# Order of the work around the sparse attention steps of a streaming encoder: minima, scaling, weight splits and gate tanh

## What is computed

```python
def sparse_attend(q, k, v, idx, valid):
    ...
    s = jnp.einsum('bqkgd,bqskd->bqkgs', qg, kg).astype(jnp.float32) * SCALE
    s = jnp.where(valid[:, :, None, None, :], s, NEG)
    p = jax.nn.softmax(s, axis=-1)
    o = jnp.einsum('bqkgs,bqskd->bqkgd', p.astype(v.dtype), vg)
    ...
merged = jax.nn.sigmoid(g_a) * br_a + jax.nn.sigmoid(g_b) * br_b + jax.nn.sigmoid(g_c) * br_c
```

## Time and profile before

| what | value |
|---|---|
| median of three runs | 1905.6 us |
| the profiled execution, its own time | 1904.03 us |
| its span, first to last instruction | 1902.2 us |
| mean granted clock of TensorE | 0.992 |
| busy: TensorE, VectorE, ScalarE, GpSimd | 96%, 57%, 32%, 21% |
| HBM traffic | 50 GB/s over the span |

### The profile page before, as it was taken

One profiled execution on the slowest core, in us unless ns is written; L12 is line 12 of the kernel. 1 busy time (PEld: TensorE's weight loads), 2 busy tenths in 40 slices (PEclk: granted clock), 3 DMA queues, 4 the chain that ended last, 5 costly groups with the idle time before them and its releaser, 6 DMA issues.

```text
span 1902.2 us, 30436 instructions
## 1 busy us (share of the span) xinstructions
PE 1835.3 (96%) x11609; PEld 1784.5 (94%) x11609; DVE 1081.7 (57%) x1749; ACT 606.2 (32%) x1006; POOL 394.8 (21%) x315
## 2 busy tenths in 40 slices
PE   5999999999999997989999999999999999999997
PEld 4899999989999996778899999999999999999997
DVE  5257878967688684778664445553234442244543
ACT  4232122268511225777723221111011111011132
POOL 2112212256533323234420001110001110011100
PEclk9999999999999998999999999999999999999998
DMA  4111111110111113211213111111111111111112
GB/s 144 34 34 48 37 34 50 49 34 24 35 49 50 37 45 100 52 40 46 56 56 136 45 34 55 44 44 44 47 42 44 44 44 55 44 34 44 43 45 92
DMA packets 167457, 96.72 MB, mean 51 GB/s; under 512 B 7676, under 2 KB 163596, under 8 KB 167372
## 3 DMA queue, kind: packets, MB, share of 16 engines
q1 hardware_dynamic: 166396, 93.57, 17.0%
q0 software_dynamic: 976, 2.00, 0.4%
HBM read 89.55 MB, written 5.99 MB: 50 GB/s over the span
## 4 chain that ended last, share of the span: by engine, by line
PE 90%; DVE 4%; ACT 2%; POOL 2%; issue 1%; DMA 1%; SPq 0%; DVEq 0%; ACTq 0%
PE ps L957 75%; PE ps L969 4%; PE ps L1066 3%; PE ps L1089 3%; PE ps L1164 2%; PE ps L1204 2%; DVE probs L2074 1%; POOL probs L829 0%; ACT w_hi L1337 0%; DVE attn_sum L2124 0%; DMA x_rows<-in_x_prompt 0%; POOL w_lo L778 0%; DMA w_raw_in_lo<-in_w_in 0%; PE ps L1030 0%; DVE h_rows L1817 0%
## 5 line engine op out<-in xcount | busy, mean ns | idle before, releaser
L957 PE MATMUL ps<-h_hi,w_hi 128*128 128x352 f32 (+1 forms) x1944 | 424.5, 327 | 3.9 <-POOL w_lo L769 3.9
L957 PE MATMUL ps<-h_hi,w_lo 128*128 128x352 f32 (+1 forms) x1944 | 419.9, 323 | 0.0
L957 PE MATMUL ps<-h_lo,w_hi 128*128 128x352 f32 (+1 forms) x1944 | 419.6, 324 | 0.0
L957 PEld LDWEIGHTS ps<-h_hi,w_hi 128*128 128x128 f32 (+1 forms) x1944 | 330.5, 189 | 6.8 <-issue 5.1
L957 PEld LDWEIGHTS ps<-h_hi,w_lo 128*128 128x128 f32 (+1 forms) x1944 | 333.6, 188 | 0.5
L957 PEld LDWEIGHTS ps<-h_lo,w_hi 128*128 128x128 f32 (+1 forms) x1944 | 330.7, 188 | 0.5
L1337 ACT ACTIVATE w_hi<-w_raw 128x1024 fp32r<-128x1024 f32 (+1 forms) x128 | 124.2, 971 | 245.6 <-PE ps L957 245.5
L926 POOL TENSOR_TENSOR t<-t,t 128x1056 f32<-128x1056 f32 x22 | 54.4, 2472 | 631.4 <-ACT t L1698 631.4
L1895 DVE MAX8 top<-key_mask 128x8 f32<-128x768 f32 (+5 forms) x192 | 170.5, 890 | 11.8 <-PE ps L957 1.1
L769 POOL TENSOR_TENSOR w_lo<-w_raw,w_hi 128x1024 fp32r<-128x1024 f32 (+1 forms) x53 | 100.5, 1896 | 355.1 <-ACT w_hi L1337 355.1
L1895 DVE MATCH_REPLACE8 key_mask<-top,key_mask 128x768 f32<-128x768 f32 (+5 forms) x192 | 167.7, 876 | 0.0
(11 more groups left out here) (261 smaller groups left out, 2975.3 us busy)
## 6 DMA issues: line engine op xcount, KB each, us to landing
w_raw_in_lo<-in_w_in SPq DMA_DIRECT2D x56, 256.0 KB, 2.8
w_raw<-in_w_in SPq DMA_DIRECT2D x54, 256.0 KB, 3.0
w_raw<-in_w_gate SPq DMA_DIRECT2D x44, 256.0 KB, 2.9
w_raw<-in_w_up SPq DMA_DIRECT2D x44, 256.0 KB, 3.0
w_raw<-in_w_down SPq DMA_DIRECT2D x32, 256.0 KB, 2.9
w_raw_in_lo<-in_w_in SPq DMA_DIRECT2D x44, 128.0 KB, 2.2
x_rows<-in_x_prompt SPq DMA_DIRECT2D x8, 512.0 KB, 8.9
w_raw<-in_w_out SPq DMA_DIRECT2D x16, 256.0 KB, 3.0
```

What stands on the lines that cost most here:

```text
L957: last = nc.tensor.matmul(PS[0:rows, NB * k + b, 0:e - a], w[:, k, t, 0:rows], x[:, t, a:e], start=m == 0 and w is WHI and x is hi, stop=m ...
```

## The change

Three loops are reordered; no instruction is added or removed.

- GpSimd: in slot c = 2, the scaling of the next pair (larger tiles) is issued ahead of the slot's weight half.
- ScalarE: within a slot, the splits and the tanh are issued last, behind `normalise`, `low_share` and `exp`. Where a pair has one chunk, both `exp` are issued in slot 0.
- VectorE: for pairs of the smaller tiles (`ahead` is 2), both `mask_max` are issued before the loop over chunks, ahead of `pt_low` and `output`; before, the second one stood in slot 1.

```diff
--- before.py
+++ after.py
@@ -902,10 +902,10 @@
             for y, pair in enumerate(SPARSE):
                 after = SPARSE[y + 1] if y + 1 < len(SPARSE) else None
                 for c in range(max(len(pair["chunks"]), 3)):
+                    if c == 2 and after and after["ahead"] == 1:
+                        normalise(after)
                     if c < len(pair["chunks"]):
                         sparse_split(y, c)
-                    if c == 2 and after and after["ahead"] == 1:
-                        normalise(after)
                 if y > 1:
                     output(SPARSE[y - 2])
             for pair in SPARSE[-2:]:
@@ -1627,15 +1627,18 @@
                     for c in range(max(count, 4)):
                         if c < count:
                             pt_high(pair, c)
-                            sparse_gates(y, c)
                         if c == 0 and after and after["ahead"] == 2:
                             normalise(after, 1)
                         if c == 0 and y > 0 and ps[y - 1]["last"]:
                             low_share(ps[y - 1])
-                        if c < 2 and ahead:
+                        if c < min(count, 2) and ahead:
                             exp(ahead, c)
+                        if c == 0 and count == 1 and ahead:
+                            exp(ahead, 1)
                         if c == 2 and after and after["ahead"] == 1:
                             normalise(after, 1)
+                        if c < count:
+                            sparse_gates(y, c)
                     if y > 0 and ps[y - 1]["last"]:
                         output(ps[y - 1])
                 low_share(ps[-1])
@@ -2147,8 +2150,11 @@
                         if early:
                             invert(after, 0)
                             invert(after, 1)
+                        if ahead and ahead["ahead"] == 2:
+                            mask_max(ahead, 0)
+                            mask_max(ahead, 1)
                         for c in range(max(count, 4)):
-                            if c < 2 and ahead:
+                            if c < 2 and ahead and ahead["ahead"] == 1:
                                 mask_max(ahead, c)
                             if c == 2 and after and not early:
                                 invert(after, 0)
```

## The result

The changed kernel takes 1921.76 us (median of four runs, 1920.9 to 1922.64) against 1905.9 for the kernel before (four runs, the three above and one of 1909.12); the ratio is 1.008 with a 95% interval of [1.0062, 1.0097]. Both the forecast (1908.6) and its range (1900.5 to 1913.5) were missed, on the slow side.

A forecast was written before the change was run, and what follows sets the result against it. TensorE, busy for 96% of the span, was taken as the bound. Smaller tiles 0.3 us gained, larger tiles 3.4 lost: 3.1 us more, put on the median of 1905.6, forecast 1908.6 us; range for 8 in 10 1900.5 to 1913.5.

The forecast's parts named there:

- the clock term of the sum: Sparse stage: a stretch of TensorE at the lower clock after a wait costs about 1.6 us; none counted in the sum.
- the slow rival: Late tanh waits: give-back fails or two to three further lower-clock stretches at 1.6 us each; about 1912.5 us, chance 0.37.
- Part 1: VectorE, smaller tiles, both minima first: at most 9.9 us of minima waits go, 0.3 us gained in all.
- step 9: Smaller tiles: splits of job 8 come late, chunk 1's fill starts at 773.9 as today; the 2.9 us gain is given back.
- step 4: Smaller tiles, before the fill of job 4: a wait of 2.46 us becomes about 2.8 for weights; gain so far 0.6.
- Step 17: Larger tiles: tanh of job 11 behind low share, exponential and split; 2.1 us lost, after give-backs 0.1 gained.
- Step 22: Larger tiles: tanh of job 14 comes behind the second exponential, after the split had moved behind the first; 1.3 us lost.
- Step 28: Larger tiles: tanh of job 19 comes behind an exponential that waits for a minimum; 1.8 us lost.
- Step 20: Larger tiles: half split moves behind an exponential, GpSimd meets it before the scaling, which ends later; 0.35 us lost.
- Steps 29 to 32: Two-chunk pairs, forecast for 29, 30, 31: tanh behind low share, half just ahead of GpSimd's scaling; together 1.55 us lost.
- The fast one: Sparse stage: minima waits go, only tanh waits replace them; 9.9 and 4.9 gained, 5 lost, about 1896 us, chance 0.19.
- The shared pair: VectorE scaling and GpSimd subtraction block each other: 0.76 us more each time; sum takes none, range one or two.

The follow-up runs named there:

- The filler: The changed kernel plus 46 unused TensorE matmuls ahead of the three waits in step 9, other engines' orders left as they are: 1913.44 us.

## Why the prediction was wrong

**The step that failed is the clock term of the sum.** The prediction said that the waits now put in place of others might "bring on further stretches", at 1.6 us each, and left them out of the sum; only the slow rival had them, two or three. There were 20.5 us more at the lower level, worth up to 10.2 us; in steps 9 and 10 alone two stretches of 6.8 us each, where the row covers 3.2. It also had no part for the stretch of 6.8 us near 722, which would have shown that one can last that long. The filler shows the price directly: 5.2 us for those two steps. Of the stage's 17.7 us the forecast had 3.1 (by its own terms 1908.7 us, written as 1908.6); of the 14.6 it lacked, 10.2 are the clock's and 4.4 are waits that were sized too small.

The sign that the prediction named for the slow rival came: the mean granted clock was 0.982 to 0.985 in the four runs, against 0.986 to 0.992 in the 38 runs of the kernel before that stand beside the experiments.

**Right, by their size and place.** Part 1 up to step 9: 2.9 us gained was forecast, and the scores of step 9 come 3.2 us earlier against the stage's start. The wait at step 4 was put at 2.8 us and is 2.61, for the half splits; at step 6 the forecast left 1.2 us (2.57 less a gain of 1.4), measured 1.40; at step 9 it comes to about 2.8 (770.7 and the row's 0.35 us of transposes to 773.9), measured 2.94. Without the clock, step 9 gave back what was forecast: of 9.7 us lost from the scores of step 9 to those of step 11, up to 6.8 are the clock's, and 2.9 are left for a forecast of 2.9. Step 17: 2.1 forecast, 2.36 measured. Step 19: 1.8, measured 2.24. Step 22: 1.3 lost forecast; the wait is 1.90 where it had been 0.43, 1.5 more, and a stretch at the lower clock stands behind it. Step 28: 1.8 lost forecast, 1.85 lost between the scores of steps 27 and 28, though only 1.22 of it is the wait for the tanh. The wait for a tanh behind a low share and the give-back of the scaling at steps 18 and 19 are as worked out. The largest tanh wait is where it was forecast (step 17, at 832); the next are those of steps 19 and 22, and not the one of step 28.

**Too small.** Without the clock's share the stage grew by 7.5 us (226.6 to 234.1), not 3.1: the smaller tiles lost 0.7 where 0.3 were to be gained, and the larger tiles lost 6.8 where 3.4 were forecast. In the smaller ones a wait of 0.65 us for the high part of the transposed probabilities (at 803.92) is new; the forecast had no late high part. Step 20: 0.35 us forecast, a wait of 1.36 for the scaling found; the queue on GpSimd was named, the exponential ahead of the split was costed too low. Steps 29 to 32: 1.55 forecast, 3.8 found from the scores of step 28 to the stage's end, of which 1.7 are the clock's (two stretches where there was one). The scaling waits are 5.7 us in all, where 4 to 5 were forecast.

**The rivals.** The slow one had the mechanism and the direction, with a chance of 0.37, and fell short by 9 us: it allowed for two or three stretches of 3.2 us, and 20.5 us more were found. The fast one ("the cover holds") fell as the text against it said: program order puts the splits behind a wait for TensorE. Its gains are real once that order is left alone: 13 us.

**The shared pair.** The prediction weighed a rule of the Trainium skill (SBUF — State Buffer, Who interferes with whom) by which a scaling on VectorE and GpSimd's subtraction block each other. In the sum it made no difference: VectorE's 17 scalings take 9.7 us in the changed kernel's stage, and took 10.1 before. Single cases agree with the rule, as the earlier trace rows does: one of 128x128 took 0.82 us at 735.54, inside a subtraction of GpSimd (734.99 to 736.27), against 0.28 alone.

What stays open is what exactly makes the clock fall. Before the change, waits of 2.01 and 1.21 us that ended 3.6 us apart (765.38 and 768.95) did not bring it down. After it, the clock fell at about 766.3, when waits of 1.27 and 0.41 us had ended 1.4 us apart (764.78 and 766.15); a third, of 0.73, came only then. And the one wait of 2.36 us in step 17 did it in two kernels and not in a third.

## What to carry to other kernels

An engine's queue is a promise about order: work that another engine needs next (a weight split, the emptying of a bank that is the only one) must not stand behind an instruction that waits for that same engine, however short that instruction is. When one wait is moved away, follow the next two instructions in the same queue that the critical engine needs, and then apply the parts of such a change one by one; here two of the three were worth 13 us and the third cost 29. Where TensorE's waits are short but close, cost the clock too, by a filler or by the stage less half of its time at the lower level.

## What the runs showed of the hardware

Idle time of TensorE can cost more than it lasts. In the changed kernel's profile two stretches of 6.8 us each at 1.2 GHz began after waits of 1.27 and 0.41 us (at 766.3) and within one of 2.94 us (774.2 to 777.13); with unused matmuls in the same waits the clock stayed at 2.4 GHz. Whether a given wait brings the clock down is not settled by its length: one of 2.36 us did in two kernels and did not in a third. Of two profiles of one kernel, one had 6.8 and the other 10.2 us at the lower level in the stage; the stage was 1.6 us longer in the second, about half of the difference.
